# Twelve query and key projections of the first layer move into its attention loop, and the loop takes its units head by head

## The reference

```python
h  = rms_norm(xl, g_pre_mix[l]) * (1.0 + sc1) + sh1       # sh1, sc1, ...: silu(c) @ w_mod[l] + b_mod[l]
u  = h @ w_glu ; u = u[..., :512] * sigmoid(u[..., 512:]) # convolution branch
u  = depthwise_conv(u, conv_w, conv_b)                    # 31 taps, then layer_norm, silu, a product
q  = (h @ w_q)   # 8 heads x 2 x 64, turned by an axial rope; the keys too
s  = einsum('bhiqd,bhikd->bhiqk', q, k) * HEAD_DIM ** -0.5
p  = softmax(s)                                           # two maps per head
a  = p[:, :, 0] - lam * p[:, :, 1]
o  = einsum('bhqk,bhkd->bhqd', a, v)                      # v: 8 heads x 128
m  = g_a * y_conv + g_b * y_attention + g_c * y_pool ; y = m @ w_out
```

## Time and profile before

| What | Value |
|---|---|
| Median of 3 runs | 2216.58 us (2215.02 to 2217.74) |
| Profiled execution, span on the page | 2206.9 us |
| Profiled execution, its own time | none is listed beside the span |
| TensorE busy | 2128.5 us, 96% |
| VectorE busy | 1442.9 us, 65% |
| ScalarE busy | 891.7 us, 40% |
| POOL busy | 178.1 us, 8% |
| Mean DMA rate over the span | 145 GB/s |

### The profile page before, as it was taken

One profiled execution on the slowest core, in us unless ns is written; L12 is line 12 of the kernel. 1 busy time (PEld: TensorE's weight loads), 2 busy tenths in 40 slices (PEclk: granted clock), 3 DMA queues, 4 the chain that ended last, 5 costly groups with the idle time before them and its releaser, 6 DMA issues. The chain is left out here.

```text
span 2206.9 us, 32856 instructions
## 1 busy us (share of the span) xinstructions
PE 2128.5 (96%) x13074; PEld 1835.4 (83%) x13074; DVE 1442.9 (65%) x2148; ACT 891.7 (40%) x1396; POOL 178.1 (8%) x251
## 2 busy tenths in 40 slices
PE   5999999999999999999999999999999999999998
PEld 3777767888888887788886998998888998898997
DVE  3487585664567766237967676875696775566764
ACT  3222374432342222235326555444455444444443
POOL 3422000010010000004310001000100000000000
PEclk9999999999999999999999999999999999999999
DMA  8544301333326666234420564776633666543663
GB/s 286 162 142 128 112 6 58 89 93 105 123 86 182 187 207 221 92 115 131 132 86 21 162 190 151 238 222 204 179 115 89 190 194 199 153 133 111 194 202 124
DMA packets 428653, 320.81 MB, mean 145 GB/s; under 512 B 25925, under 2 KB 379702, under 8 KB 428502
## 3 DMA queue, kind: packets, MB, share of 16 engines
q1 hardware_dynamic: 425408, 310.52, 46.6%
q0 software_dynamic: 2656, 8.03, 1.3%
q10 hardware_dynamic: 438, 0.17, 0.0%
HBM read 317.62 MB, written 1.05 MB: 144 GB/s over the span
## 5 line engine op out<-in xcount | busy, mean ns | idle before, releaser
L344 DVE TENSOR_TENSOR split<-raw,split 128x1024 fp32r<-128x1024 f32 (+1 forms) x382 | 459.6, 1208 | 368.1 <-ACT split L341 367.1
L355 PE MATMUL PS<-HH,split 128*128 128x256 f32 (+1 forms) x1752 | 585.0, 334 | 4.0 <-DVE HL L2212 1.7
L357 PE MATMUL PS<-HH,split 128*128 128x256 f32 (+1 forms) x1752 | 573.7, 327 | 0.0
L356 PE MATMUL PS<-HL,split 128*128 128x256 f32 (+1 forms) x1752 | 573.5, 327 | 0.0
L341 ACT ACTIVATE split<-raw 128x1024 fp32r<-128x1024 f32 (+1 forms) x382 | 389.5, 1034 | 363.0 <-PE PS L357 325.6
L355 PEld LDWEIGHTS PS<-HH,split 128*128 128x128 f32 x1752 | 329.1, 188 | 42.5 <-issue 10.2
L356 PEld LDWEIGHTS PS<-HL,split 128*128 128x128 f32 x1752 | 329.3, 188 | 31.2 <-issue 1.0
L357 PEld LDWEIGHTS PS<-HH,split 128*128 128x128 f32 x1752 | 329.0, 188 | 31.3
L355 PE MATMUL PS<-HH,apart 128*128 128x256 f32 x800 | 228.7, 286 | 16.9 <-DVE HL L495 11.7
L356 PE MATMUL PS<-HL,apart 128*128 128x256 f32 x800 | 224.8, 281 | 0.0
L357 PE MATMUL PS<-HH,apart 128*128 128x256 f32 x800 | 224.6, 281 | 0.0
(11 more groups left out here) (340 smaller groups left out, 3076.6 us busy)
## 6 DMA issues: line engine op xcount, KB each, us to landing
raw<-in_w_in_dram SPq DMA_DIRECT2D x120, 512.0 KB, 4.2
raw<-in_w_ffn_in_dram SPq DMA_DIRECT2D x88, 512.0 KB, 4.8
raw<-in_l_w_gate_up_dram SPq DMA_DIRECT2D x88, 512.0 KB, 3.9
G<-in_w_mod_dram SPq DMA_DIRECT2D x82, 512.0 KB, 4.0
raw<-in_w_ffn_out_dram SPq DMA_DIRECT2D x44, 512.0 KB, 3.5
raw<-in_l_w_down_dram SPq DMA_DIRECT2D x44, 512.0 KB, 4.6
raw<-in_l_w_in_dram SPq DMA_DIRECT2D x28, 512.0 KB, 3.9
raw<-in_w_attn_out_dram SPq DMA_DIRECT2D x16, 512.0 KB, 4.0
```

The source lines that it names most:

```text
L344: eng.tensor_tensor(c["low"], c["raw"], c["high"].bitcast(F32), ALU.subtract).then_inc(low_done, 1)
L355: pe.matmul(out, a[0], b[0], start=first, stop=False)
L356: pe.matmul(out, a[0], b[1], start=False, stop=False)
L357: return pe.matmul(out, a[1], b[0], start=False, stop=last)
```

## The change

In the first layer only two query tiles and two key tiles (heads 0 and 1) stay ahead of the loop. The other twelve tiles are put into the loop, one to a double step, query and key of a head in turn, between the scores and the transposes of that step; the rope's swap matmul of a tile is the first thing of the next double step. ScalarE cuts and copies these tiles between the exponentials and the copies of the transposes, VectorE cuts the low parts behind the maxima.

In both layers units go head by head (`for h ... for t ...`), so widths of 512 and 256 keys alternate in the first layer. Both transposes now stand ahead of both value products. Scores have four banks instead of six, transposes two instead of one, and the filling tiles and their ropes share one bank (`FILL`).

A modulation row chunk now stands at every point from 0 to 23 instead of two of three, so that all 24 still lie ahead of the loop; the second transposition of rows follows point 18. Of the convolution's taps VectorE makes two groups of four beside each of the first four ropes and four groups beside the value chunks, and the rest in the loop, half ahead of each step's first `probs` and half behind it. O, MT, MTL and MTH trade places in memory, the attention output is kept head by head, the rope's scratch and its grid lie in `XN` in the first layer, whose grid load waits for the last transposes of the first norm, and VectorE waits for the pooled sums ahead of the ropes.

```diff
-S_BANKS, PAIR_BANKS, ONE_PT_BANK, FOUR_O_BANK = (0, 1, 2, 3), (0, 1, 2, 3, 4, 5), (6,), (7,)
+S_BANKS, PAIR_BANKS, TURN_BANKS, FOUR_O_BANK, FILL = (0, 1, 2, 3), (0, 1, 2, 3), (4, 5), (6,), (7,)
...
-    turn_points = {"start": {11: groups[0]}, "L0_proj": {13: groups[2], 25: groups[3]}}
+    turn_points = {"start": {11: groups[0]}, "L0_proj": {13: groups[2], 18: groups[3]}}
...
-        if phase == "L0_proj":
-            q = 2 * (point // 3) + point % 3 if point % 3 < 2 else None
-        else:
-            q = point
-        return q if q is not None and 0 <= q < KT * len(phases[phase]) else None
+        return point if 0 <= point < KT * len(phases[phase]) else None
...
-    ROPES = [("q", j) for j in range(8)] + [("k", j) for j in range(8)]
-    units_of = {l: [(t, h) for t in layer_tokens(l)[2] for h in range(HEADS)] for l in range(DEPTH)}
+    FIRST_HEADS = {0: 2, 1: HEADS}
+    ahead_ropes = {l: [(nm, h) for nm in ("q", "k") for h in range(FIRST_HEADS[l])] for l in range(DEPTH)}
+    filled = {l: [(nm, h) for h in range(FIRST_HEADS[l], HEADS) for nm in ("q", "k")] for l in range(DEPTH)}
+    ropes_of = {l: ahead_ropes[l] + filled[l] for l in range(DEPTH)}
+    units_of = {l: [(t, h) for h in range(HEADS) for t in layer_tokens(l)[2]] for l in range(DEPTH)}
...
             def behind_values(c):
-                mod_pe(T, pe, L + "proj", 28 + c)
+                mod_pe(T, pe, L + "proj", 12 + 2 * heads + c)
...
+            def fill(step):
+                if step < len(filled[l]):
+                    nm, h = filled[l][step]
+                    c0, rhs, width = (COL_Q, own, n) if nm == "q" else (COL_K, all_tokens, 2 * SEQ)
+                    c, ws = T.load(rows(w_in, 0, KT, c0 + h * P, P), (KT, P), columns=width)
+                    tile_t(T, pe, (L + nm, h), ws, KT, 0, rhs, width, FILL)
+                    T.used(c)
+
             for i in range(0, len(us) + 4, 2):
+                step = i // 2
+                if 0 < step <= len(filled[l]):
+                    turn(*filled[l][step - 1], FILL)
                 if i < len(us):
                     scores(i)
                     scores(i + 1)
...
+                fill(step)
+                if 2 <= i < len(us) + 2:
+                    turned(i - 2)
+                    turned(i - 1)
                 if i >= 4:
                     weighted(i - 4)
-                if 2 <= i < len(us) + 2:
-                    turned(i - 2)
-                if i >= 4:
                     weighted(i - 3)
-                if 2 <= i < len(us) + 2:
-                    turned(i - 1)
@@ ScalarE @@
+            for i in range(0, len(us) + 4, 2):
+                step = i // 2
+                if step < len(filled[l]):
+                    split_until(act, (L + filled[l][step][0], filled[l][step][1]))
                 if i < len(us):
+                    exps(i)
+                    exps(i + 1)
+                if step < len(filled[l]):
+                    projected(*filled[l][step])
                 if 2 <= i < len(us) + 2:
+                    copy_turned(i - 2)
+                    copy_turned(i - 1)
+                if i >= 4 and i % 4 == 2:
+                    copy_out((i - 3) // 4)
@@ POOL @@
-            for i, (nm, j) in enumerate(ROPES):
+            for i, (nm, j) in enumerate(ropes_of[l]):
@@ VectorE @@
+            dve.wait_ge(S(L + "pooled"), 4)
+            for i, rope in enumerate(ahead_ropes[l]):
                 rope_sin(*rope)
-                mod_dve(dve, L + "proj", 12 + i)
-                for _ in range(2 if l and i >= 6 else 1):
+                if l == 0 and i in (1, 3):
+                    mod_dve(dve, L + "proj", {1: 13, 3: 18}[i])
+                for _ in range(2 if l == 0 or i >= 6 else 1):
                     conv_step()
...
+            else:
+                for i in range(4):
+                    conv_step()
+                    split_until(dve, (L + "v", 1, 3), i - 4)
+                last_taps = [x for a, tap, b, late in both_taps for x in ((a, tap), (b, late))] + last_taps
...
-            for i in range(len(us) + 1):
+            for i in range(0, len(us), 2):
+                step = i // 2
+                if 0 < step <= len(filled[l]):
+                    rope_sin(*filled[l][step - 1])
+                maxes(i)
+                maxes(i + 1)
...
+                if step < len(filled[l]):
+                    split_until(dve, (L + filled[l][step][0], filled[l][step][1]))
+                    for one in last_taps[step * per_step:step * per_step + per_step // 2]:
+                        conv_taps(*one)
+                probs(i)
+                if step < len(filled[l]):
+                    for one in last_taps[step * per_step + per_step // 2:(step + 1) * per_step]:
+                        conv_taps(*one)
+                probs(i + 1)
```

More of the change, by code:

```diff
@@ L682, in norm_pe @@
             pe.wait_ge(S(name + "_xn"), n + 1)
-            transposes(T, pe, name, tiles[n], XN[:, n % 2, :])
+            transposes(T, pe, name, tiles[n], [XN[:, n % 2, k * P:(k + 1) * P] for k in range(KT)])
     def transposes(T, pe, name, t, src):
@@ L743, in build @@
     at_o = place[0]
-    O = over(at_o, "O", [P, 4, D])
+    O = over(at_q, "O", [P, HEADS, 4, V_DIM])
     place[0] += 2 * D * 4
@@ L1358, in scores @@
                 t, h = us[i]
+                if t == 0:
+                    for nm in ("q", "k"):
+                        pe.wait_ge(S(L + nm + "_roped"), max(h + 1, heads) if l else h + 1)
                 k0, k1 = (0, 2 * SEQ) if t < 2 else (SEQ, 2 * SEQ)
@@ L1432, in _ @@
                 pe.wait_ge(S(L + "o_normed"), t + 1)
-                transposes(T, pe, L + "ot", t, O[:, t, :])
+                transposes(T, pe, L + "ot", t, [O[:, h, t, :] for h in range(HEADS)])
             branch(L + "yb", 2, 1, A["w_attn_out"][l], 8, (OTH, OTL), lambda: pe.wait_ge(S(L + "ot_parts"), 2 * len(tiles)))
@@ new lines, in exps @@
+            def exps(i):
+                t, h = us[i]
+                w = 2 * SEQ if t < 2 else SEQ
+                act.wait_ge(S(L + "maxes"), i + 1)
+                if i >= 2:
+                    act.wait_ge(S(L + "probs"), i - 1)
+                for m in range(2):
+                    key = (L + "s", i, m)
+                    read_out(act.activation(E2[:, i % 2, m, 0:w], bank(key)[:, 0:w], ACT.Exp, bias=mx[:, i % 2, m:m + 1],
+                                            scale=-1.0, accum_out=mx[:, i % 2, 5:6] if m else sum0[:, t, h:h + 1]), key)
@@ new lines, in copy_turned, with copy_out @@
+            def copy_turned(i):
+                w = 2 * SEQ if us[i][0] < 2 else SEQ
+                key = (L + "pt", i)
+                wait_result(act, key)
+                if i >= 2:
+                    wait_result(act, (L + "head", i - 2))
+                read_out(act.activation(AT[:, i % 2, 0:w], bank(key)[:, 0:w], ACT.Copy), key)
+            def copy_out(o):
+                per = 4 // len(tiles)
+                key = (L + "o", o)
+                wait_result(act, key)
+                read_out(act.activation(O[:, per * o:per * (o + 1), 0:len(tiles), :],
+                                        bank(key).rearrange("p (h t d) -> p h t d", h=per, t=len(tiles)), ACT.Copy), key)
@@ L1700, in _ @@
                 wait_result(pool, key)
-                pool.tensor_tensor(x, x, grid[:, 0, :], ALU.mult).then_inc(pool_step, 1)
+                pool.tensor_tensor(x, x, grids[l][:, 0, :], ALU.mult).then_inc(pool_step, 1)
                 count["pool"] += 1
```

133 lines of the change are left out of this document (55 added, 78 removed).

## The result

The changed kernel takes 2225.27 us, median of 5 runs (2220.78 to 2228.11), beside 2216.58 (2211.41 to 2218.05, 5 runs) for the kernel before. The medians stand as 1.0039 to 1; the ratio on record is 1.005, 95% interval 1.0028 to 1.0072. The change is slower by 8.7 us. The forecast was 2215.5, no change that can be measured, and the time lies above its range of 2209 to 2223.5.

The account below looks back on a forecast made before the run. TensorE, busy 96%, was taken to bound the kernel, so its waits count. -71.0 + 5.3 + 2.2 + 61.9 + 0.5 = -1.1 us on a span of 2206.9, plus 9.7, gave 2215.5 us; range 2209 to 2223.5.

Parts of the forecast that it names:

- The third row chunk: Ahead of the first loop: its load waits for a ring slot, TensorE stands 3.65 us, half clock costs 1.7; together +5.3.
- The wait for value chunk 5: Ahead of the first loop: VectorE's taps and split take 15.4 us against TensorE's 13.15, so TensorE waits 2.2 us.
- the tiles and turns that left: Ahead of the first loop: twelve tiles at 5.44 us and twelve rope turns at 0.48 leave, 71.0 us less.
- Loop: 135.85: First layer's attention loop with the tiles filled in: 135.85 us instead of 73.9, to the stage's end +61.9.
- So 0.2 a head is lost where taps run: Filled steps: VectorE's rope sine frees the shared bank at tile end + 4.2, TensorE reaches it at + 3.99.
- The bare 19.2: Filled pair of steps, one head: TensorE's work without waits or changes between kinds of matmul, 19.2 us; bounds 19.0 and 19.6.
- stays within DVE's 1.4 us of slack in a step: Filled steps: POOL's rope slows VectorE's four taps by some 0.9 us, which the step's slack absorbs; counted as 0.
- the third rival: Filled steps: POOL's two rope instructions wholly block VectorE, 1.85 us a step; 0.6 a head more, 2218.5 us; chance 0.18.
- with the drain 20.1: End of the first loop: the last four steps, without tiles, follow the softmax chain and take 20.1 us including the drain.
- the second layer, forecast +0.5: Second layer's loop: steps 5.25 instead of 5.17 (+0.6), bank wait +0.6, drain gives 0.7 back; +0.5, bounds 0 and 2.
- Rival 2: Unfilled steps of both loops: ScalarE's copies fall on the softmax chain, steps grow to about 6.2; +11 us, 2226.5; chance 0.15.
- the excess of 9.7 us: Whole kernel: the median 2216.58 lay 9.7 us above the profiled span 2206.9, and the forecast kept this on top.

Follow-up runs that it names:

- the other bank: Several mends combined, plus four-unit outputs returned to the bank that rotating tiles never use and the bank rotation set on ahead of mixing: 2207.67 us, 0.9971 to the kernel before.
- the turned rotation: Bank rotation set on by two per filled tile, ahead of the mixing matmuls (0.9971 to the kernel before) or, in a later kernel, behind the first layer's loop (0.9963).

## Why the prediction was wrong, point by point

Before the loop the sum held. Forecast -63.5, measured -63.0 (the mixing matmuls start at 204.69 instead of 267.35, the row chunks 0.37 later). The third row chunk cost 6.6 instead of 5.3: the wait was 3.65 to the hundredth, the half clock behind it lasted 6.8 us instead of 3.4 and cost 2.9 instead of 1.7. Since it lasted 3.4 in five other kernels with the same wait, and the chunk cost about 5.4 in four of them, the term was right, and the 1.3 belong to the clock of the execution as far as these profiles show. The wait for value chunk 5 cost 1.7 with a small one before it (1.33 and 0.21 in the trace, the rest in the spacing of the row chunks), forecast 2.2. The rest, the tiles and turns that left, is 71.3 by difference, forecast 71.0.

The step that failed is the loop: "Loop: 135.85", measured 142.9. Three terms of it were mis-sized or missing.

First, "So 0.2 a head is lost where taps run". It was about 0.8: the pair is 20.04 instead of 19.4, five pairs 100.05 instead of 97.0, above the 19.6 that the prediction took for its upper bound of a pair. The chain itself (taps, second probability, sine, the one shared bank) was right: with F the tile's end, 255.75, TensorE reached the bank at F + 3.9, forecast 3.99, but had it at F + 4.66, forecast 4.2. The bare 19.2 was right too, since that is what the pair takes in the two kernels without the wait. The price of POOL in the chain was set at nothing, with the sentence that its slowing "stays within DVE's 1.4 us of slack in a step". A slack of a whole step does not help where the instruction that is slowed stands between the transposes and the bank. This is close to the third rival: POOL in VectorE's way, and 0.6 a head on top of 0.2. But it is one POOL instruction ahead of one bank and not both of them on a VectorE that is full. The Trainium skill, SBUF — State Buffer, section Who interferes with whom, had been weighed only as a rival, on the strength of the earlier trace rows; the traces of the changed kernel and of the one with the later POOL agree with it on which instructions meet, and show less than a wait for the whole one: 0.5 us for a product of 0.72, 0.4 for an overlap of 0.53, nothing for the maxima that read PSUM. The row that was weighed against it was misread. Beside its four taps POOL made two rope instructions, and these are longer too; alone one takes 0.73. POOL in the kernel before:

```profile
136.09 1.11 POOL L1705 TENSOR_TENSOR QT<-QT,TMP 128x256 f32<-128x256 f32 x1 [5.64 <-DVE TMP L1780]
137.16 1.18 POOL L1701 TENSOR_TENSOR QT<-QT,TMP 128x256 f32<-128x256 f32 x1
...
174.10 0.73 POOL L1701 TENSOR_TENSOR QT<-QT,TMP 128x256 f32<-128x256 f32 x1 [2.50 <-PE PS L711]
```

So VectorE's 0.9 us were half of the delay, and the other half, 0.8, was on POOL. The 1.85 us of the earlier trace rows hold such a delay already (the 1.11 there).

Second, the end: "with the drain 20.1", measured 23.9. From the first maximum of step 12 (328.70) to the last probability (346.71) the chain takes 18.0 us, about what its steps gave. The drain behind it takes 4.6 (to 351.33), where the kernel before takes 1.7 from its last probability at 343.10 to 344.81. Two things are in it: ScalarE copies the transposes of two units only behind all four exponentials of the next two (TensorE waits 1.59 for that at 346.31), and the first tile of the next stage needs the bank whose outputs ScalarE still copies, 0.78. The old order gave back 2.0 with the 0.78 still in it; the other bank took that. The remaining 1.0 of the 3.8 is not explained.

Third, the second layer, forecast +0.5, measured +2.7 to +3.1 in two profiles. Its steps of 5.26 were right. The start (0.66 for the bank, then a third score pair that waits 1.20 for exponentials, with four banks instead of six) and the drain (1.90 of waiting against 0.69) were priced too low: 0.6 for the bank was near, the wait of the third pair has no price in the sum, and the drain was to give 0.7 back. The old order with its six banks gave back all but the 0.7 of the first scores, and the turned rotation that too. That this loop moved by more than 2 us is one of the prediction's own signs of being wrong.

Together 1.3 - 0.5 - 0.3 + 7.1 + 2.4 = 10.0 us more than the -1.1 forecast: +8.9, measured 8.7 between the medians. That they agree so closely is partly luck, as the 1.3 show. Rival 2, copies of ScalarE on the softmax chain in the unfilled steps, forecast 11 us; steps of 5.26 and 3.6 from maximum to maximum (337.77 to 343.03, 334.16 to 337.77) speak against it. The copies that hold TensorE up by more than a microsecond stand in the drains, so its time, 2226.5, was met by other causes. The absolute forecast stood on the median before, since the excess of 9.7 us was carried on whole. That excess is not time around the span: in the second profile of the kernel before, 9.5 us longer, the added time lies behind the second layer's loop (11.6 us there, 2.1 less ahead of it). Some 8.7 of the 11.6 are clock, an estimate from 17.3 us more at half clock there; the rest is open.

## What to carry to other kernels

Work moved into a stage with idle time is paid by that stage's chain, not by its engines' slack: follow each moved instruction to the buffer that it holds and ask what is queued between the last event and its release. Here a shared bank cost 4.8 us and a plain change of order in the loop 3.6 and 2.0, while the filling itself gained; with these mended, and the third row chunk moved, +0.5% became -0.3% to -0.4%. And a drain deserves its own count, since every pairing that helps in steady steps is paid there once.

## What the runs showed of the hardware

A product on VectorE with both inputs in SBUF and a product on POOL run side by side only for a small part: 0.75 became 1.25 us beside 0.72 of POOL, 1.21 became 1.61 beside an overlap of 0.53. Either engine can be the one that pays: in the kernel before, POOL's sum of 170.49 took 1.11 us beside taps that had begun first, and 0.74 at 141.17, where it began ahead of a tap. The delay shows as a longer instruction and not as idle time ahead of it.

The clock falls in stretches that depend on more than the program: in the kernel before, the stretch near 1655 us ran at 1.00 in one execution and at 0.50 for 13.6 us in another, with 2218.19 us for the second. Over the whole span half clock adds up to about 41 and 48 us in the two profiles of the kernel before, and to 58 and 55 in those of the changed kernel. Profiles of single executions of this kernel differ by as much as the change is worth, so stages were compared by the starts of the same instruction, and totals by medians only.
